# Layer 1 attention of an fp32 encoder trunk: its output is made turned, with V stationary and in rounded parts, and stored so

## The reference

```python
def _gqa_axial(h, w_qkv, g_qn, g_kn, w_o, row, col):
    b, s, _ = h.shape
    proj = h @ w_qkv
    q = proj[..., :HB * HD].reshape(b, s, HB, HD)
    k = proj[..., HB * HD:(HB + KVB) * HD].reshape(b, s, KVB, HD)
    v = proj[..., (HB + KVB) * HD:].reshape(b, s, KVB, HD)
    q = _axial_rope(_rms(q, g_qn), row, col)
    k = _axial_rope(_rms(k, g_kn), row, col)
    o = _block_attention(q, k, v, HD ** -0.5)
    return o.reshape(b, s, HB * HD) @ w_o
```

## Time and profile before

| | |
|---|---|
| runs | 2411.65, 2409.13, 2412.70 us; median 2411.65 |
| profiled execution: span | 2406.4 us |
| PE busy | 2205.8 us (92%) |
| DVE, ACT, POOL busy | 1613.7 (67%), 1261.6 (52%), 545.4 us (23%) |
| attention of layer 1, steady part | 1145 to 1580 us of the span |
| output stage of layer 1, first load to the last tile's projection | 1588.5 to 1779.4 us |

### The profile page before, as it was taken

How to read it: one execution, slowest core, us unless ns; L and a number is a source line. 1 busy time by engine, 2 the same in 40 slices (tenths; PEclk the granted TensorE clock), 3 DMA queues, 4 the chain that set the end, 5 groups by cost and what they waited for, 6 DMA issues and landing times. The chain is left out here.

```text
span 2406.4 us, 32340 instructions
## 1 busy us (share of the span) xinstructions
PE 2205.8 (92%) x11028; PEld 1677.9 (70%) x11028; DVE 1613.7 (67%) x1832; ACT 1261.6 (52%) x1486; POOL 545.4 (23%) x430
## 2 busy tenths in 40 slices
PE   8899998969999999977899999969969999999993
PEld 5677776747777777746788888757756777777772
DVE  3566664578888888855566566552258888888883
ACT  3444443157777777743443434341107777777772
POOL 1100000012234233205232222200000332344222
PEclk9999998979999999987999999989979999999997
DMA  7000004769999999934111112152169999999983
GB/s 264 1 14 8 13 14 156 280 228 378 385 385 378 396 382 383 351 95 135 36 49 49 49 48 61 56 191 88 70 245 342 382 381 389 390 380 383 393 295 126
DMA packets 169530, 520.40 MB, mean 216 GB/s; under 512 B 11808, under 2 KB 49440, under 8 KB 169184
## 3 DMA queue, kind: packets, MB, share of 16 engines
q1 hardware_dynamic: 162272, 494.05, 54.4%
q0 software_dynamic: 7168, 25.17, 4.5%
HBM read 481.43 MB, written 37.75 MB: 216 GB/s over the span
## 5 line engine op out<-in xcount | busy, mean ns | idle before, releaser
L1764 DVE TENSOR_TENSOR m_w_lo<-s_raw,m_w_hi 128x2048 fp32r<-128x2048 f32 x384 | 865.9, 2288 | 144.6 <-ACT m_w_hi L1713 143.0
L1713 ACT ACTIVATE m_w_hi<-s_raw 128x2048 fp32r<-128x2048 f32 x384 | 731.1, 1916 | 175.9 <-PE m_ps_down L1809 77.3
L1807 PE MATMUL m_ps_gate<-m_w_hi,m_xeT_hi 128*96 128x512 f32 x512 | 206.0, 402 | 3.8 <-DVE m_xeT_lo L1770 3.8
L1807 PE MATMUL m_ps_down<-m_w_hi,m_hidT_hi 128*96 128x512 f32 x512 | 203.9, 398 | 3.8 <-DVE m_hidT_lo L1770 3.8
L1809 PE MATMUL m_ps_gate<-m_w_hi,m_xeT_lo 128*96 128x512 f32 x512 | 204.3, 399 | 0.0
L1809 PE MATMUL m_ps_down<-m_w_hi,m_hidT_lo 128*96 128x512 f32 x512 | 204.1, 399 | 0.0
L1807 PE MATMUL m_ps_up<-m_w_hi,m_xeT_hi 128*96 128x512 f32 x512 | 203.9, 398 | 0.0
L1684 POOL DMA_INDIRECT acc<-m_ye,m_row_scatter x32 | 47.0, 1469 | 688.4 <-ACT m_ye L1730 688.4
L1809 PE MATMUL m_ps_up<-m_w_hi,m_xeT_lo 128*96 128x512 f32 x512 | 202.7, 396 | 0.0
L1808 PE MATMUL m_ps_gate<-m_w_lo,m_xeT_hi 128*96 128x512 f32 x512 | 202.5, 395 | 0.0
L1808 PE MATMUL m_ps_down<-m_w_lo,m_hidT_hi 128*96 128x512 f32 x512 | 202.3, 395 | 0.0
(11 more groups left out here) (228 smaller groups left out, 4200.4 us busy)
## 6 DMA issues: line engine op xcount, KB each, us to landing
s_raw<-in_w_gate SPq DMA_DIRECT2D x128, 1024.0 KB, 7.6
s_raw<-in_w_up SPq DMA_DIRECT2D x128, 1024.0 KB, 7.3
s_raw<-in_w_down SPq DMA_DIRECT2D x128, 1024.0 KB, 7.8
s_raw<-in_w_qkv_b SPq DMA_DIRECT2D x16, 512.0 KB, 5.8
s_raw<-in_w_qkv_b SPq DMA_DIRECT2D x32, 256.0 KB, 6.1
s_raw<-in_w_o_b SPq DMA_DIRECT2D x1, 8192.0 KB, 23.2
acc<-o_x SPq DMA_DIRECT2D x12, 512.0 KB, 2.6
xn<-o_xn SPq DMA_DIRECT2D x12, 512.0 KB, 3.0
```

What stands on the lines that cost most here:

```text
L1713: act.activation(hi[:, split, :, :].rearrange("p k n -> p (k n)"), raw[:, slot, :], ACT.Copy).then_inc(hi_ready, 1)
L1764: dve.tensor_tensor(lo[:, split, :, :].rearrange("p k n -> p (k n)"), raw[:, slot, :], hi[:, split, :, :].rearrange("p k n -> p (k n)"), A ...
L1807: pe.matmul(out[:, cols], left_hi[:, k, :], hi[:, split, kk, cols], start=(k == 0), stop=False)
```

## The change

A new class `TurnedCore` takes the place of `Core` in `gqa_block` (`Core` stays for layer 0). The probabilities are multiplied by 1/row sum in SBUF before they are turned (`dve_scale`). The turned probabilities are split in hi (ACT) and lo (DVE), both query tiles of a unit side by side, and so is V. The products have V stationary and 256 columns of probabilities moving, and leave the output turned: head dimension on partitions, queries in columns. It is written into the bank of `T` in which the turned probabilities of j = 1 lay, split (`act_out`, `dve_out`) into a ring of 4 buffers, and stored by unit (256 KB, hi and lo) into `oT_b`. POOL multiplies the gains by 1/rms for each tile (`scale`) instead of multiplying the tables beforehand. The output stage of layer 1 loads a tile (2 MB, hi and lo) and multiplies it directly; its y has two buffers.

```diff
     def pe_turn(self, pe, n, unit, ident):
         _, nk = keys_of(unit)
         for j in range(2):
-            pe.wait_ge(self.exp_done, 2 * n + j + 1)
-            wait(pe, self.out_done, 2 * n - 1 + j)
+            pe.wait_ge(self.scaled, 2 * n + j + 1)
+            if j == 0:
+                wait(pe, self.pT_split, 2 * n - 1)
+            else:
+                wait(pe, self.oT_split, n)
             for k in range(nk):
                 last = pe.transpose(self.T[:, j, k, :], self.probs[:, unit % 2, j, k * P:(k + 1) * P], ident)
             last.then_inc(self.turned, 1)
 
-    def pe_pv(self, pe, n, unit, v_of):
+    def pe_pv(self, pe, n, unit, v_hi, v_lo):
+
         key, nk = keys_of(unit)
-        for j in range(2):
-            pe.wait_ge(self.copied_act if j == 0 else self.copied_dve, n + 1)
-            for k in range(nk):
-                last = pe.matmul(self.T[:, j, 0, 0:self.dv], self.probsT[:, j, k, :], v_of(key + k),
-                                 start=(k == 0), stop=(k == nk - 1))
-            last.then_inc(self.pv_done, 1)
+        pe.wait_ge(self.pT_split, 2 * n + 2)
+        out = self.oT[0:self.dv]
+        for k in range(nk):
+            pe.matmul(out, v_hi(key + k), self.pT_hi[:, k, :, :], start=(k == 0), stop=False)
+            pe.matmul(out, v_hi(key + k), self.pT_lo[:, k, :, :], start=False, stop=False)
+            last = pe.matmul(out, v_lo(key + k), self.pT_hi[:, k, :, :], start=False, stop=(k == nk - 1))
+        last.then_inc(self.pv_done, 1)
...
-    def act_copy(self, act, n, unit):
+    def act_high(self, act, n, unit):
         _, nk = keys_of(unit)
-        act.wait_ge(self.turned, 2 * n + 1)
-        wait(act, self.pv_done, 2 * n - 1)
-        act.activation(self.probsT[:, 0, 0:nk, :], self.T[:, 0, 0:nk, :], ACT.Copy).then_inc(self.copied_act, 1)
+        wait(act, self.pv_done, n)
+        for j in range(2):
+            act.wait_ge(self.turned, 2 * n + j + 1)
+            act.activation(self.pT_hi[:, 0:nk, j, :], self.T[:, j, 0:nk, :], ACT.Copy).then_inc(self.pT_high, 1)
+
+    def act_out(self, act, n, ring):
+        act.wait_ge(self.pv_done, n + 1)
+        if not (isinstance(n, int) and n < self.RING):
+            act.wait_ge(self.stored[ring], n * 4 - ring * 4)
+        act.activation(self.out[0:self.dv, ring, :, 0, :], self.oT[0:self.dv], ACT.Copy).then_inc(self.oT_high, 1)
...
-    def dve_copy(self, dve, n, unit):
+    def dve_low(self, dve, n, unit):
         _, nk = keys_of(unit)
-        dve.wait_ge(self.turned, 2 * n + 2)
-        wait(dve, self.pv_done, 2 * n)
-        dve.tensor_copy(self.probsT[:, 1, 0:nk, :], self.T[:, 1, 0:nk, :]).then_inc(self.copied_dve, 1)
-
-    def dve_rinv(self, dve, n, unit):
+        for j in range(2):
+            dve.wait_ge(self.pT_high, 2 * n + j + 1)
+            dve.tensor_tensor(self.pT_lo[:, 0:nk, j, :], self.T[:, j, 0:nk, :], self.pT_hi[:, 0:nk, j, :],
+                              ALU.subtract).then_inc(self.pT_split, 1)
+
+    def dve_scale(self, dve, n, unit):
+
+        _, nk = keys_of(unit)
         dve.wait_ge(self.exp_done, 2 * n + 2)
-        wait(dve, self.out_done, 2 * n)
+        wait(dve, self.scaled, 2 * n - 2)
         dve.reciprocal(self.rinv[:, unit % 2, :], self.rowsum[:, unit % 2, :]).then_inc(self.rinv_done, 1)
-
         dve.wait_ge(self.rinv_done, n + 1)
         for j in range(2):
+            at = self.probs[:, unit % 2, j, 0:nk * P]
+            dve.tensor_scalar(at, at, self.rinv[:, unit % 2, j:j + 1], None, ALU.mult).then_inc(self.scaled, 1)
+
+    def dve_out(self, dve, n, ring):
+        dve.wait_ge(self.oT_high, n + 1)
+        dve.tensor_tensor(self.out[0:self.dv, ring, :, 1, :], self.oT[0:self.dv], self.out[0:self.dv, ring, :, 0, :],
+                          ALU.subtract).then_inc(self.oT_split, 1)
+
+
+
+    def store(self, sp, n, unit, ring, chunk, rows):
+
+        tile, _ = UNITS[unit]
+        sp.wait_ge(self.oT_split, n + 1)
+        sp.dma_start(self.oT_dram[tile:tile + 2, rows, chunk, :].rearrange("t p k n -> p t (k n)"),
+                     self.out[0:self.dv, ring, :, :, :].rearrange("p t c n -> p t (c n)").bitcast(F32)
+                     ).then_inc(self.stored[ring], 16)
...
+            store(GROUPS - 2, 0)
             sp.wait_ge(proj_done, NU * GROUPS)
             sp.dma_start(shared.w_o_b, io.w_o_b[0].rearrange("(k p) n -> p k n", p=P)).then_inc(shared.w_o_landed, 16)
-            core.store(sp, GROUPS - 2, 0)
-            core.store(sp, GROUPS - 1, 1)
-            for slot in range(2):
-                sp.wait_ge(core.stored[slot], 16 * GROUPS // 2)
+            store(GROUPS - 1, 1)
+            for ring in range(core.RING):
+                sp.wait_ge(core.stored[ring], 16 * GROUPS * NU // core.RING)
...
             def tile(m, t):
 
                 pool.wait_ge(mean_ready, m + 1)
                 wait(pool, normed_ready, m)
                 pool.tensor_tensor(rstd[:, t % 2, :], mean[:, t % 2, :], half[:, :], ALU.pow).then_inc(rstd_ready, 1)
                 pool.wait_ge(rstd_ready, m + 1)
+                pool.tensor_tensor(scale[:, :, :], gains[:, :, :],
+                                   rstd[:, t % 2, :].unsqueeze(2).to_broadcast([P, 3, HD]),
+                                   ALU.mult).then_inc(scale_ready, 1)
+                pool.wait_ge(scale_ready, m + 1)
                 wait(pool, qkT_done, m - 1)
-                pool.tensor_tensor(normed[:, t % 2, :, :], raw[:, t % 2, :, :],
-                                   rstd[:, t % 2, :].unsqueeze(2).to_broadcast([P, 3, HD]),
+                pool.tensor_tensor(normed[:, t % 2, :, :], raw[:, t % 2, :, :], scale[:, :, :],
                                    ALU.mult).then_inc(normed_ready, 1)
                 pool.wait_ge(normed_ready, m + 1)
                 wait(pool, roped_ready, m)
-                pool.tensor_tensor(straight[:, :, :], normed[:, t % 2, :, :], tables[:, t, 0, :, :],
+                pool.tensor_tensor(straight[:, :, :], normed[:, t % 2, :, :],
+                                   rope[:, t, 0, :].unsqueeze(1).to_broadcast([P, 3, HD]),
                                    ALU.mult).then_inc(straight_ready, 1)
...
 
             norm.pool_tile(pool, 0, half[:, 0:1])
             norm.pool_tile(pool, 1, half[:, 0:1])
-            pool.wait_ge(tables_landed, 48)
-            for h in range(3):
-                table(h)
-                norm.pool_tile(pool, 2 + h, half[:, 0:1])
-            norm.pool_tile(pool, TILES - 1, half[:, 0:1])
-            pool.wait_ge(tables_ready, 5 * 3)
+            pool.wait_ge(tables_landed, 64)
             for t in range(TILES):
+                if t + 2 < TILES:
+                    norm.pool_tile(pool, t + 2, half[:, 0:1])
                 tile(t, t)
...
-            def squared(m, t):
+            def squared(m, slot, t):
                 dve.wait_ge(sq_ready, m + 1)
                 wait(dve, mean_ready, m - 1)
                 dve.tensor_reduce(ssq[:, t % 2, :], squares, AX.X, ALU.add).then_inc(ssq_ready, 1)
+                dve.wait_ge(v_ready, m + 1)
+                dve.tensor_tensor(V_lo[:, slot, t, :], core.proj[:, t % 2, 3 * HD:], V_hi[:, slot, t, :],
+                                  ALU.subtract).then_inc(v_split, 1)
                 dve.wait_ge(ssq_ready, m + 1)
                 wait(dve, rstd_ready, m - 1)
                 dve.tensor_scalar(mean[:, t % 2, :], ssq[:, t % 2, :], 1.0 / HD, EPS,
...
             core.dve_max(dve, 1, 1)
+            core.dve_scale(dve, 0, 0)
             split_low(1, 1, 0)
...
-                    core.dve_copy(dve, n, unit)
-                    core.dve_rinv(dve, n, unit)
+                    core.dve_low(dve, n, unit)
                     if unit == 0:
                         rotate(g * NU + TILES - 1, TILES - 1)
                     elif not last:
...
                     if unit == 0:
                         turned(g, slot, TILES - 1, core.proj)
                     if not last:
-                        squared(g * NU + NU + unit, unit)
+                        squared(g * NU + NU + unit, 1 - slot, unit)
                         if unit:
                             turned(g + 1, 1 - slot, unit - 1, core.proj)
-                    core.dve_out(dve, g, n, unit, slot, first or (isinstance(g, int) and g < 2))
+                    if not (last and unit == NU - 1):
+                        core.dve_scale(dve, n + 1, (unit + 1) % NU)
+                    core.dve_out(dve, n, (slot * NU + unit) % core.RING)
                     if not (last and unit >= NU - 2):
                         core.dve_max(dve, n + 2, (unit + 2) % NU)
...
+                if STORED_TURNED:
+                    wait(sp, y_done, 2 * i - 2)
+                    sp.dma_start(oT[:, i % 2, :, :, :].rearrange("p k c n -> p (k c n)").bitcast(F32),
+                                 io.oT_b[ORDER[i]].rearrange("p k n -> p (k n)")).then_inc(o_landed[i % 2], 16)
+                    return
...
+                if part == 0 and STORED_TURNED:
```

(42 more changed lines are left out.)

193 lines of the change are left out of this document (135 added, 58 removed).

## The result

The changed kernel takes 2394.65 us (median of four runs, 2394.06 to 2398.57) where the kernel before takes 2410.41 in the same comparison: ratio 0.9938, interval 0.9924 to 0.9952. A second comparison on another occasion gave 0.9949 (0.9937 to 0.9961). So it is 12 to 15 us faster; the forecast was 12, from 2411.65 to 2400. The profiled spans are 2406.4 and 2396.8.

The account below looks back on a forecast made before the run. PE was taken to bound layer 1's attention (busy 418.6 of 435.0 us). Steady steps +7, split steps +8, last group +8, prologue -4, output stage -31 make -12: from 2411.65 to 2400 us, range 2384 to 2420.

Parts of the forecast that it names:

- The output stage: Layer 1's output stage: first tile loaded turned and split, no transposes or wait for DVE's low part; -31 us.
- The steady attention: Steady attention steps: PE's turn waits for DVE's scaling and dve_out; +7 us over seven groups, split steps +8 more.
- The walk of DVE's chain: Steady attention, z the start of products with V: scaling from z+2.19, dve_out, next projection at z+3.76.
- the split steps at +8: Attention steps with a weight split, 12 in all: DVE's split waits for POOL, PE stalls; +8 us, bounds 0 and 11.
- all attention waits are hidden: Rival, attention: DVE gets the scaling out early and splits pass POOL; 2375 us, chance .08.
- The prologue: Prologue: POOL's 15 table multiplications go, so norms stop waiting behind them; -4 us, between -6.4 and +4.
- The last group: Last attention group: nothing projected, bare chain, sample units 5.8 us for 4.67, prompt units half the rise; +8 us.
- That rival (2433): Rival, attention: POOL's operation issued at z+1.6 holds both scalings until it ends, 1.0 us later; 2433 us, chance .12.
- The second rival: Rival, attention: POOL gets between the two scalings, second half .85 us later in units 1 to 4; 2416 us, chance .14.
- The fourth, the plain rate: Rival, attention: the scaling runs at DVE's plain rate, .69 us for 512 columns; 2410 us, chance .10.

Follow-up runs that it names:

- y_single: The changed kernel with one buffer of y in the output stage, as before the change: 2398.8 us, ratio 0.996 to the kernel before.
- early_scale: The changed kernel with dve_scale moved up in DVE's order, to right behind the rotation: 2376.03 us, ratio 0.9867 to the kernel before.
- output_only: The kernel before with the changed output stage, its attention output stored unturned, twice (wrong in layout): 2375.73 us, ratio 0.9863 to the kernel before.
- after_again: The changed kernel unaltered, measured again: 2396.2 us, ratio 0.9949 to the kernel before.
- norms_first: The changed kernel with POOL's input norm of tile t+3, not t+2, ahead of the chain of tile t: 2391.31 us, ratio 0.9929 to the kernel before.
- v_low_again: The changed kernel with only V's low part moved, to behind dve_out, run a second time: 2398.13 us, ratio 0.9959 to the kernel before.

## Why the prediction was right, step by step

**The output stage** was right in mechanism and size: -32.1 for -31. The load and the tiles came out as worked out, no new wait appeared, and y_single shows that the second buffer of y had no part in it, which leaves the transposes and their wait.

**The steady attention** was right in sum (+13.6 for +7 and +8), and in mechanism for the scaling (PE waits for L432 and L436), but two terms were mis-sized against each other. The walk of DVE's chain ended with the projection at z+3.76; it is z+3.99. Of the .23, .12 are the two scalings (.88 together where I had .76; one takes .484 where I took .43), .05 their later start (z+2.24) and the rest the hand-over from L436 to PE. From z to the projection units 1 to 5 are .79, .02, .02, .70 and .67 us longer than before, 2.2 a group where I had .95, and unit 0, which I put at nothing, is .26 longer. The way from a projection to the next products is .08 shorter in each of the six steps (5.91 for 5.99), which leaves the 1.94 a group, within .03. The other term, **the split steps at +8**, failed in its step "I let the split wait for POOL too": it was read off L1041 in the earlier trace rows, where POOL had been first. Here DVE was first in all 12, POOL waited, and PE did not: two signs that the prediction named, L1141 starting at the end of L1054 and PE's L1254 waiting after units 2 and 4, did not come. That I gave two thirds to the wrong order is why the sum fits; it is luck, not working. Two of its sums are off besides, by 1 us each: two thirds of .9 is .6, so that 12 splits make 7 and not 8, and 3.2 x 7 is 22 and not 23.

That the wait is one for the order, not for the work, is shown by early_scale: the same instructions, 2.8 us a group less. Then .9 of the products' saving of 1.46 a group is there (56.4 for 57.2); unit 4's split takes .4 of the rest. The prediction had this only as a rival ("all attention waits are hidden", 2375), which it held against the late place of the scaling; the place is one that a moved call changes, and the kernel then takes 2376.

**The prologue** at -4 failed: -0.1 in the profiles. The pair of profiles with 64 in that row (output_only and after_again) says the same, +.2. The step that failed was that the tables' work goes and the norms come earlier. They hardly do for the last tiles: behind the first projection, ACT's copy of tile 5 starts after 47.5 us in output_only, 46.7 in after_again and 40.7 in norms_first. POOL's tile chains now stand ahead of the norms of tiles 3 to 5, which I had priced only as the bad end of the bounds. norms_first shows the 5 us behind it.

**The last group** (+9.0 for +8; +7.8 in after_again) was right in mechanism, and its terms are off both ways. Three successive sample units begin their products at

```profile
1586.30 0.39 PE L373 MATMUL b_ps_probsT<-b_pT_hi,b_V_hi 128*128 128x256 f32 x1 [1.84 <-DVE b_pT_lo L420]
...
1592.08 0.39 PE L373 MATMUL b_ps_probsT<-b_pT_hi,b_V_hi 128*128 128x256 f32 x1 [1.83 <-DVE b_pT_lo L420]
...
1599.40 0.45 PE L373 MATMUL b_ps_probsT<-b_pT_hi,b_V_hi 128*128 128x256 f32 x1 [1.84 <-DVE b_pT_lo L420]
```

```profile
1592.00:1598.00 6.00, 5.49 (x26) 4.74 (x26) 2.73 (x7) 1.48 (x5) 0.00 (x0) 0.72 0.81 294
```

The first takes 5.78, as worked out. The second takes 7.32, with the clock at .72, partly at the lower of its two levels (1.2 and 2.4 GHz), after a unit in which PE had stood idle for 1.84. Unit 0, a prompt unit, grew from 3.7 to 6.5 us, where I had given it half of 1.13. Against that the last two units together, up to the load, grew only from 10.6 to 11.8, where I had 3.3. So the sum comes near by terms that balance.

**The rivals.** POOL's L1043 does not hold the scalings: in the step of unit 4 above, L432 starts .48 after it, while it runs, and takes .88 for two, its usual time. That rival (2433) fell. The Trainium skill, "SBUF — State Buffer", section "Who interferes with whom", says that a DVE instruction with two SBUF inputs contends with a GpSimd one that reads SBUF, and that between DVE in its two-port modes and GpSimd whoever issues first gets the shared pair of ports for the whole instruction. The trace agrees for L1141 against L1054 (3.03 us for 1.0) and not for L1043 beside L432. The two do meet there, but it is POOL that pays: L1043 takes 1.01 in that step, and .85 in each of the 42 steps of early_scale from 1145 us on, where the scalings stand elsewhere. The second rival, POOL between the two scalings, does happen in v_low_again (four times, 1.46 for two, the step .8 longer where the prediction priced .85), but not once in the profile of the changed kernel, whose L432 averages .484 and is never over .492. The fourth, the plain rate, fell: 512 columns take .484 us and 256 take .351, .52 ns for each column more, where L420, with one operand in PSUM, takes .678 and .409, 1.05 ns.

## What to carry to other kernels

When work moves ahead of a step that another engine waits for, ask at what time its input is ready and where its place in that engine's order is; here the exponentials lay ready for 5.6 us (unit 5's ended at 1436.10, their scaling began at 1441.70), and one moved call was worth more than the whole change. Price the parts of a change apart: 33 us won in one stage and some 20 lost in another look like a modest gain. Of two engines that share a resource, work out which one issues first before charging the wait to either.

## What had not been expected of the hardware

POOL pays as readily as DVE: an operation of 1.0 us took 3.03 behind a DVE split issued .14 us earlier. And identical prologue code differs by 3 us from one profiled execution to another (67.2 and 64.0 to group 1 with the prologue of before, 67.1 and 64.2 with the changed one). PE's clock goes with it. The prologue of the changed kernel, in its first profile and in after_again:

```profile
1096.00:1163.00 67.00, 55.14 (x234) 44.12 (x235) 34.56 (x62) 24.82 (x50) 25.37 (x32) 0.86 0.30 91
```

```profile
1097.40:1161.50 64.10, 52.25 (x234) 41.67 (x235) 34.58 (x62) 25.04 (x50) 25.40 (x32) 0.90 0.30 95
```

The granted clock is .86 and .90, and PE is busy for 55.1 and 52.3 us with the same work; the other engines' busy times are equal. So a term of 3 us can't be read from one pair of profiles before their clocks are compared.
